# Expert-choice search in two halves of the latent tokens and the context side by side, with jobs of the attention and router stages in a new order (2 layers, float32, one core)

## The reference

```python
def trunk_layer(x, cvec, lp, lam_init, ctx_kv):
    mod = silu(cvec) @ lp['w_ada'] + lp['b_ada']            # 6 x 1024
    sh1, sc1, g1, sh2, sc2, g2 = split(mod, 6)
    h = rms_norm(x, lp['rms1_g']) * (1 + sc1) + sh1
    q, k, v, up, uc = split(h @ lp['w_in'])                 # 8 heads, 2 x 64 for q and k, 128 for v
    ...                                                     # q, k normed; rotary on latent tokens
    y_a = differential attention @ w_proj_a; y_b = pooling @ w_proj_b; y_c = convolution @ w_proj_c
    x = x + g1 * ((ga * y_a + gb * y_b + gc * y_c) @ lp['w_out'])
    h2 = rms_norm(x, lp['rms2_g']) * (1 + sc2) + sh2
    return x + g2 * expert_choice_ffn(h2, ...)

def expert_choice_ffn(h, w_router, w1, w3, w2):             # 16 experts, width 1024
    aff = softmax(h @ w_router)
    gate, idx = top_k(swapaxes(aff, 1, 2), cap)             # cap 64 of 512 latent, 16 of 128 context tokens
    xs = h[idx]
    ye = ((silu(xs @ w1) * (xs @ w3)) @ w2) * gate
    return scatter-add of ye at idx
```

## Time and profile before

| | |
|---|---|
| median of 3 runs | 2980.21 us (2978.73 to 2989.21) |
| the profiled execution | 2972.85 us, of which the span 2971.1 us |
| granted TensorE clock, mean | 0.973 of full speed |
| PE / PEld busy | 93% / 75% |
| DVE / ACT / POOL busy | 66% / 52% / 12% |
| chain that ended last | PE 68%, DMA 14%, DVE 8%, ACT 5%, issue 3% |
| stages of layer 0 (us) | start and input to 184, attention to 516, merge to 806, projection to 872, router to 920, experts to 1474 |
| stages of layer 1 (us) | attention 1644 to 1972, merge to 2262, projection to 2329, router to 2381, experts to 2938, end at 2971 |

### The profile page before, as it was taken

The page is one execution under the profiler, slowest core; times in us unless marked ns, Lnnn a source line. Parts: engine busy times, 40 slices in busy tenths (PEclk is TensorE's granted clock), DMA queues, the critical chain, the costliest instruction groups (busy, mean ns, idle before and its releaser), DMA issues.

```text
span 2971.1 us, 42113 instructions
## 1 busy us (share of the span) xinstructions
PE 2764.0 (93%) x17280; PEld 2238.3 (75%) x17280; DVE 1957.4 (66%) x2015; ACT 1547.5 (52%) x1993; POOL 365.4 (12%) x235
## 2 busy tenths in 40 slices
PE   6999997999988999999989999989999599999998
PEld 5988876999975666666679788779999466666666
DVE  2165656873438888888843666577534588888886
ACT  5235545324227777777642455543232377777774
POOL 0410110000011211111123011100000201111110
PEclk8999999999998999999999999989999799999999
DMA  7222232222268999999932233122232499999996
GB/s 242 89 85 90 93 92 80 70 80 100 79 221 306 374 375 372 373 375 375 341 125 72 79 107 103 51 90 82 67 104 100 165 316 374 375 371 374 375 372 239
DMA packets 373999, 605.63 MB, mean 204 GB/s; under 512 B 13040, under 2 KB 164720, under 8 KB 373040
## 3 DMA queue, kind: packets, MB, share of 16 engines
q1 hardware_dynamic: 360496, 551.67, 52.6%
q0 software_dynamic: 13312, 51.28, 5.6%
HBM read 572.62 MB, written 30.28 MB: 203 GB/s over the span
## 4 chain that ended last, share of the span: by engine, by line
PE 68%; DMA 14%; DVE 8%; ACT 5%; issue 3%; SPq 1%; DVEq 0%; ACTq 0%; POOLq 0%
PE ps L1351 20%; PE ps L1353 19%; PE ps L1352 19%; DMA m_raw<-in_w 11%; DVE m_lo L1271 2%; PE ps L1542 2%; PE ps L1575 2%; DMA raw<-in_w_ada 1%; ACT probs L546 1%; PE ps L1395 1%; DVE stats L1059 1%; PE ps L1564 1%; DMA xg<-h_rows,token_of_slot 1%; SPq L332 1%; DVE stats L1030 1%
## 5 line engine op out<-in xcount | busy, mean ns | idle before, releaser
L834 ACT CAST m_hi<-m_raw 128x2048 fp32r<-128x2048 f32 x384 | 732.9, 1912 | 292.5 <-DMA m_raw<-in_w 275.5
L1271 DVE TENSOR_TENSOR m_lo<-m_raw,m_hi 128x2048 fp32r<-128x2048 f32 x384 | 861.7, 2284 | 18.0 <-PE ps L1353 12.5
L1351 PE MATMUL ps<-h_hi,w_hi 128*128 128x384 f32 (+2 forms) x1408 | 439.5, 312 | 16.7 <-DVE h_lo L983 9.4
L1352 PE MATMUL ps<-h_lo,w_hi 128*128 128x384 f32 (+2 forms) x1408 | 436.8, 310 | 0.0
L1353 PE MATMUL ps<-h_hi,w_lo 128*128 128x384 f32 (+2 forms) x1408 | 436.8, 310 | 0.0
L1351 PE MATMUL ps<-m_hi,xs_hi 128*80 128x512 f32 x1024 | 406.1, 397 | 3.4 <-DVE xs_lo L1288 3.4
L1352 PE MATMUL ps<-m_lo,xs_hi 128*80 128x512 f32 x1024 | 403.8, 394 | 0.0
L1353 PE MATMUL ps<-m_hi,xs_lo 128*80 128x512 f32 x1024 | 403.2, 394 | 0.0
L1351 PE MATMUL ps<-w_hi,h_hi 128*128 128x256 f32 x960 | 283.0, 295 | 2.8 <-ACT pool_branch L673 1.8
L1351 PEld LDWEIGHTS ps<-h_hi,w_hi 128*128 128x128 f32 x1408 | 267.6, 190 | 22.0 <-issue 21.9
L1352 PE MATMUL ps<-w_lo,h_hi 128*128 128x256 f32 x960 | 273.7, 285 | 0.0
(11 more groups left out here) (292 smaller groups left out, 4632.7 us busy)
## 6 DMA issues: line engine op xcount, KB each, us to landing
m_raw<-in_w SPq DMA_DIRECT2D x384, 1024.0 KB, 10.3
raw<-in_w_in SPq DMA_DIRECT2D x72, 512.0 KB, 6.4
raw<-in_w_ada SPq DMA_DIRECT2D x64, 512.0 KB, 4.7
raw<-in_w_gate SPq DMA_DIRECT2D x48, 512.0 KB, 4.7
ada_in_a<-in_w_ada SPq DMA_DIRECT2D x10, 1024.0 KB, 11.9
raw<-in_w_proj_a SPq DMA_DIRECT2D x16, 512.0 KB, 4.0
raw<-in_w_out SPq DMA_DIRECT2D x16, 512.0 KB, 5.7
x_kept<-x POOLq DMA_DIRECT2D x2, 2560.0 KB, 10.4
```

The costliest lines, as they stand in the source:

```text
L834: nc.scalar.copy(m_hi[:, g % HIS], m_raw[:, g % RAWS]).then_inc(s["m_high"], 1)
L1271: nc.vector.tensor_tensor(m_lo[:, g % LOS], m_raw[:, g % RAWS], m_hi[:, g % HIS].bitcast(F32), ALU.subtract).then_inc(s["msplit"], 1)
L1351: pe.matmul(out, wh, xh, start=first, stop=False, skip_group_check=True)
L1352: pe.matmul(out, wh, xl, start=False, stop=False, skip_group_check=True)
```

## The change

- **Job tables, loads.** `a1` moves from the end of tile 3 to tile 4, behind the turns and the first part's scores; `v1` or `v4` moves from ahead of the turns to the place where `a1` was. In the last head all four modulation jobs come one or two tiles later. SP asks for the next head's chunks between the two modulation chunks of a head, no longer ahead of both.
- **Start of layer 0.** `ada_turned` runs in three parts among the last two chunks; `split_low(0, 0)` comes behind `add_mods` and `coefficients`.
- **Last chunk of the output projection.** Its second tile's third piece goes to bank 2, TensorE reports each tile by itself, VectorE and ScalarE take the first while the second is computed. A one-column exponential stands behind the root. VectorE fills four tiles with constants.
- **Search.** The affinities are laid out in 32-wide groups (two divisions instead of one) so that two transposes put the first 256 latent tokens on partitions 0 to 15, the other 256 on 32 to 47, the context on 64 to 79. Eight rounds run over 80 partitions by 256 columns. The two latent lists are laid against each other, the second reversed; after two transposes of 80 rows the larger value at each of the 64 places is taken, with its token. The 64 are then the right set, no longer in falling order.
- **Order behind the search.** On TensorE the wait for the search and the two transposes (now into bank 6, behind the wait for the last token rows' copies) come ahead of `ada_turned(l + 1, 4)`. On VectorE the three `low` come ahead of the next layer's `add_mods` and `coefficients`.

```diff
-EVEN = (("", "q1", "q2"), ("", "q3", "q4"), ("", "v0", "a0"), ("", "b0", "a1"), ("v1 tq tk tc", "", "Q0 b1"))
-ODD = (("", "q1", "q2"), ("", "q3", "q4"), ("", "v2", "a0"), ("", "v3", "b0 a1"), ("v4 tq tk tc", "", "Q0 b1"))
-LASTH = (("", "a0", ""), ("", "b0", "a1"), ("", "b1", ""), ("", "", ""), ("", "", ""))
+EVEN = (("", "q1", "q2"), ("", "q3", "q4"), ("", "v0", "a0"), ("", "b0", "v1"), ("tq tk tc", "a1", "Q0 b1"))
+ODD = (("", "q1", "q2"), ("", "q3", "q4"), ("", "v2", "a0"), ("", "v3", "b0 v4"), ("tq tk tc", "a1", "Q0 b1"))
+LASTH = (("", "", ""), ("", "a0", ""), ("", "b0", ""), ("", "a1", "b1"), ("", "", ""))
...
-                for h in range(HEADS):
+
+                def tiles_of(h):
+
                     if h % 2 == 0 and h < HEADS - 2:
                         wide(0, in_v[l, h // 2 + 1 + V0 // CW])
                     if h < HEADS - 2:
                         qk_chunk(h + 2)
                     elif h == HEADS - 2:
                         wide(0, gate_v[l, MERGE[0][1] + 4 * MERGE[0][0]])
-                    for a in (ADA0 + 2 * h + 1, ADA0 + 2 * h + 2):
-                        if a < 24:
-                            ada_chunk(a)
+
+                tiles_of(0)
+                for h in range(HEADS):
+                    ada_chunk(ADA0 + 2 * h + 1)
+                    tiles_of(h + 1)
+                    if h < HEADS - 1:
+                        ada_chunk(ADA0 + 2 * h + 2)
...
-                    squares(2 * c, 2 * c + 2)
-                seen("proj", 4)
+                    squares(2 * c, 2 * c + (1 if c == 3 else 2))
+                act.wait_ge(s["xo_done"], seen("xo_done"))
+                squares(KT - 1, KT)
+                seen("proj", 5)
 
                 root_of_rows()
+                nc.scalar.activation(st[:, 6:7], ones[:, 0:1], ACT.Exp)
...
-                    split_low(0, 0)
                     add_mods(0, 0)
                     coefficients(0, 8, "rms1")
+                    split_low(0, 0)
...
+                    if c == 3:
+                        nc.vector.memset(affw[:], -1.0)
+                        nc.vector.memset(top_f[:], 0.0)
+                        nc.vector.memset(top_w[:], 0.0)
+                        link(nc.vector.memset(aff_lanes[:], 0.0))
                     for j in range(2):
                         ct = 2 * c + j
+                        third = 2 if (c, j) == (3, 1) else 3 * u + 2
+                        if c == 3:
+                            dve.wait_ge(s["proj"], seen("proj"))
                         for col, a, e in ((1, 0, 3 * P), (1, 3 * P, LAT), (0, LAT, TOK)):
-                            src = ps[:, 3 * u + j, 0:3 * P] if a == 0 else ps[:, 3 * u + 2, 256 * j + a - 3 * P:256 * j + e - 3 * P]
+                            src = ps[:, 3 * u + j, 0:3 * P] if a == 0 else ps[:, third, 256 * j + a - 3 * P:256 * j + e - 3 * P]
                             ins = nc.vector.scalar_tensor_tensor(x[:, ct, a:e], src,
                                                                  mods_of[l][:, 16 + ct, col:col + 1], mm_[:, ct, a:e], ALU.mult, ALU.add)
+                        if (c, j) == (3, 0):
+                            seen("xo_done")
+                            ins.then_inc(s["xo_done"], 1)
...
-                nc.vector.tensor_tensor(aff[:], aff[:], st[:, 8:13].unsqueeze(2).to_broadcast([P, TT, EXPERTS]), ALU.mult).then_inc(s["aff_r"], 1)
+                turn = st[:, 8:13].unsqueeze(2).to_broadcast([P, TT, EXPERTS])
+                nc.vector.tensor_tensor(aff_lanes[:, 0:3, 0:EXPERTS], aff[:, 0:TT:2], turn[:, 0:TT:2], ALU.mult)
+                nc.vector.tensor_tensor(aff_lanes[:, 3:TT, 0:EXPERTS], aff[:, 1:TT:2], turn[:, 1:TT:2], ALU.mult).then_inc(s["aff_r"], 1)
...
-                nc.vector.tensor_copy(affw[:], flat[0:EXPERTS, 5 * 512:5 * 512 + TOK]).then_inc(s["aff_in"], 1)
+                nc.vector.tensor_copy(affw[0:64], ps[0:64, 5, 0:LAT // 2])
+                nc.vector.tensor_copy(affw[64:LANES, 0:CTX], ps[64:LANES, 5, 0:CTX]).then_inc(s["aff_in"], 1)
                 dve.wait_ge(s["aff_in"], seen("aff_in"))
-                for a, b, at, rounds in ((0, LAT, 0, CAP_LAT // 8), (LAT, TOK, CAP_LAT, CAP_CTX // 8)):
-                    for i in range(rounds):
-                        best = top_v[:, at + 8 * i:at + 8 * i + 8]
-                        link(nc.vector.max(best, affw[:, a:b]))
-                        link(nc.vector.max_index(top_i[:, at + 8 * i:at + 8 * i + 8], best, affw[:, a:b]))
-                        if i < rounds - 1:
-                            link(nc.vector.match_replace(affw[:, a:b], best, affw[:, a:b], -1.0))
-                nc.vector.tensor_copy(top_f[:, 0:CAP_LAT], top_i[:, 0:CAP_LAT])
-                nc.vector.tensor_scalar(top_f[:, CAP_LAT:], top_i[:, CAP_LAT:], float(LAT), None, ALU.add).then_inc(s["topk"], 1)
+                for i in range(CAP_LAT // 8):
+                    best = top_v[:, 8 * i:8 * i + 8]
+                    link(nc.vector.max(best, affw[:]))
+                    link(nc.vector.max_index(top_i[:, 8 * i:8 * i + 8], best, affw[:]))
+                    if i < CAP_LAT // 8 - 1:
+                        link(nc.vector.match_replace(affw[:], best, affw[:], -1.0))
+                nc.vector.tensor_copy(top_w[0:EXPERTS, 0:CAP_LAT], top_v[0:EXPERTS])
+                nc.vector.tensor_copy(top_w[32:32 + EXPERTS, 0:CAP_LAT], top_v[32:32 + EXPERTS, ::-1])
+                nc.vector.tensor_copy(top_w[64:LANES, CAP_LAT:], top_v[64:LANES, 0:CAP_CTX])
+                nc.vector.tensor_copy(top_f[0:EXPERTS, 0:CAP_LAT], top_i[0:EXPERTS])
+                nc.vector.tensor_scalar(top_f[32:32 + EXPERTS, 0:CAP_LAT], top_i[32:32 + EXPERTS, ::-1], float(LAT // 2), None, ALU.add)
+                nc.vector.tensor_scalar(top_f[64:LANES, CAP_LAT:], top_i[64:LANES, 0:CAP_CTX], float(LAT), None, ALU.add).then_inc(s["topk"], 1)
                 dve.wait_ge(s["posT"], seen("posT"))
-                nc.vector.tensor_copy(index[:], ps[0:SLOTS, 7, 0:EXPERTS])
-                nc.vector.tensor_copy(st[0:SLOTS, 62:63], ps[0:SLOTS, 7, EXPERTS - 1:EXPERTS])
-                nc.vector.tensor_copy(gates[:], ps[0:SLOTS, 7, EXPERTS:2 * EXPERTS]).then_inc(s["routed"], 1)
+                placed = ps[0:SLOTS, 6, 0:2 * LANES].rearrange("p (n c) -> p n c", n=2)
+                value_a, token_a = placed[0:CAP_LAT, 0, 0:EXPERTS], placed[0:CAP_LAT, 1, 0:EXPERTS]
+                value_b, token_b = half_b[:, 0], half_b[:, 1]
+                link(nc.vector.tensor_copy(half_b[:], placed[0:CAP_LAT, :, 32:32 + EXPERTS]))
+                nc.vector.tensor_tensor(a_or_b[:], token_a, token_b, ALU.subtract)
+                link(nc.vector.tensor_tensor(from_a[:], value_a, value_b, ALU.is_ge))
+                nc.vector.tensor_copy(token_f[CAP_LAT:], placed[CAP_LAT:, 1, 64:LANES])
+                link(nc.vector.tensor_tensor(a_or_b[:], a_or_b[:], from_a[:], ALU.mult))
+                link(nc.vector.tensor_tensor(token_f[0:CAP_LAT], a_or_b[:], token_b, ALU.add))
+                nc.vector.tensor_copy(index[:], token_f[:])
+                nc.vector.tensor_copy(st[0:SLOTS, 62:63], token_f[:, EXPERTS - 1:EXPERTS])
+                nc.vector.tensor_tensor(gates[0:CAP_LAT], value_a, value_b, ALU.max)
+                nc.vector.tensor_copy(gates[CAP_LAT:], placed[CAP_LAT:, 0, 64:LANES]).then_inc(s["routed"], 1)
...
+                dve.wait_ge(s["h2_out"], seen("h2_out", 16 * TT))
+                for g in range(AHEAD_LO):
+                    low(g)
                 if l < DEPTH - 1:
                     dve.wait_ge(s["small_in"], seen("small_in", 32))
                     add_mods(l + 1, 4)
                     coefficients(l + 1, 8, "rms1")
-                dve.wait_ge(s["h2_out"], seen("h2_out", 16 * TT))
-                for g in range(AHEAD_LO):
-                    low(g)
...
-                    ada_first(6, 8)
-                    ada_turned(0, 0)
+                    ada_turned(0, 0, 0, 2)
+                    ada_first(6, 7)
+                    ada_turned(0, 0, 2, 3)
+                    ada_first(7, 8)
+                    ada_turned(0, 0, 3, 4)
...
+                        if (c, j) == (3, 1):
+                            seen("proj")
+                            ins.then_inc(s["proj"], 1)
+                            pe.wait_ge(s["set_free0"], seen("set_free0", 0) + 1)
...
-                for c in range(TT):
-                    ins = pe.transpose(flat[0:EXPERTS, 5 * 512 + c * P:5 * 512 + (c + 1) * P], aff[:, c, :], ident[:])
+                pe.transpose(ps[0:96, 5, 0:P], aff_lanes[:, 0:3].rearrange("p t e -> p (t e)"), ident[:])
+                ins = pe.transpose(ps[0:64, 5, P:2 * P], aff_lanes[:, 3:TT].rearrange("p t e -> p (t e)"), ident[:])
...
+                pe.wait_ge(s["topk"], seen("topk"))
+                pe.wait_ge(s["h2tok"], seen("h2tok", 2))
+                seen.settle()
+                pe.transpose(ps[0:SLOTS, 6, 0:LANES], top_w[:], ident[0:LANES, 0:LANES])
```

(7 more changed lines are left out.)

34 lines of the change are left out of this document (22 added, 12 removed).

## The result

The changed kernel takes 2966.43 us (median of six runs, 2959.58 to 2972.10) where the kernel before, in six runs of the same measurement, takes 2985.55: 19.1 us less, a ratio of 0.9933 with a 95% interval of 0.9918 to 0.9949. The forecast was 18.6 us less and 2961.6 us. The total agrees, but three of its five terms don't: what two of them had too much is made good by a gain that the sum held open and by a rest that no stage explains.

The account below looks back on a forecast made before the run. TensorE was taken to bound the stages, with transfers at full share among the experts and sequential waits between stages. Start 4.4, attention 5, gather starts 5.1 and 4.1 made 18.6 us off 2980.21: 2961.6 us, range 2950 to 2977.

Parts of the forecast that it names:

- a gain that the sum held open: First gathers of the expert stages: one short and one long kept as before, 0 in the sum, bounds -5.5 and +5.5.
- The start: Layer 0's start: early turns fill waits, first modulated tile 4.4 us earlier; 1.5 if the clock falls before 37.
- Attention: Both layers' attention: moved jobs and loads remove waits for modulation chunks; 5 us gained, ends -1 and 10.
- the second rival: Attention: rotation replaces the chunk's wait and the clock falls there too; gain 0, total 2966.6 us; chance 0.13.
- The fear about SP's order: Heads 2 and 4, both layers: first modulation chunk asked for late, could wait; slower, 2995 us; chance 0.06.
- From the projection to the search: Each layer, end of output projection: split handover and early table load bring all that follows 3.0 us earlier.
- The search: Each layer's token search: 256-column maxima at 0.415 us; 7.9 of 19.2 us goes, six closing copies add 0.35.
- What is late then: Into the gathers: token-row stores decide, not the search; gather starts 5.1 us earlier in layer 0, 4.1 in layer 1.
- The gather's length: First gather of each layer, 8.05 and 13.61 us before: either length possible in either; one short, one long kept.
- The first rival: Both gathers alike: both long 2967.1 us, chance 0.10; both short 2956.1 us, chance 0.27.
- The sum: Whole kernel: 4.4 + 5 + 5.1 + 4.1 = 18.6 us gained, taken from the median, giving 2961.6 us.
- The premise: Expert stage: TensorE busy 544 of 554 us, transfers at full share; earlier first product brings the end forward as much.

Follow-up runs that it names:

- jobs_as_before: Changed kernel with the job tables and SP's load order of the kernel before put back: 2966.68 us, ratio to before 0.9940.
- rows_first: Changed kernel; layer 0's fourth to sixth expert chunk held until the gather landed, low parts until its issue, rows' low part and cast earlier: 2965.95 us.

## Why the prediction came out right, step by step

- **The start: right.** 4.4 us forecast, 4.6 measured at the first modulated tile, 3.9 between the second traces of the two kernels (46.73 and 42.84); at the first scores 4.6 and 3.2. The condition held too: the clock was still full during the early turns, 1.84 us for 16 of them, and, which the sum had not assumed, even at chunk 7.
- **Attention: wrong, 5 us forecast, none found.** The working of layer 1's head 0 was right: the turns start 38.17 us after the head's first scores instead of 38.85, and the head takes 40.65 instead of 41.30. What failed is the rest of the sum, which counted the half clock behind the old waits as saved. The new waits, for the rotation, are as long, and the clock falls as often (a mean of 0.94 to 0.97 over the stages of both traces before, 0.92 to 0.96 after): that is the second rival. It came true in full; that the measured time also meets its total, 2966.6 us, is luck, since that total has the other wrong terms in it. The prediction also left the last row of the table without a price. Counted from first scores to first scores, the first seven heads of both layers take 609.0 us together in the four traces with the old tables and 604.1 in the seven with the new ones (those averaged for `jobs_as_before`); the last heads take it back, 57.5 us and 64.0. These hold one modulation chunk more (161 products instead of 145), which now runs behind the boundary, and in the first traces their clock is 0.74 and 0.80 instead of 0.94 and 0.81. The fear about SP's order did not come true: no modulation chunk was late.
- **From the projection to the search: right in kind, 3.0 forecast.** Updates 2.18 to 1.14, squares 1.36 to 0.74, and from the last subtraction's start (879.65) to the exponential's 0.33 us instead of 1.61: 2.9 together. The stretch in the table got another 0.9 shorter, in TensorE's small steps between, which I did not cost: behind a wait of 0.87 us for ScalarE's square, which had been 2.54, they ran at a granted clock of 0.95 (874 to 880 us) instead of 0.53 (873 to 880).
- **The search: right, and in the shade as forecast.** 0.424 us for a maximum against 0.415 estimated; from the first maximum's start to the last index's start 11.1 us instead of 18.9. It is not the search that releases the gathers.
- **What is late then: right in layer 1, wrong in layer 0.** In layer 1 from the first update to the gather's start 83.17 became 78.93, 4.2 us against 4.1 forecast (5.1 between the second traces), released by the last store as worked out. In layer 0 84.24 became 82.78: 1.5 instead of 5.1 (1.7 between the second traces). The step that failed is "lands a median 3.5 later (3.0 to 4.2)". That landing time was read where the expert chunks had all but arrived; moved ahead, the last store is issued 6.6 us before the sixth chunk lands, and takes 8.39. In every trace with the changed order the landing stays 34.2 to 34.5 us behind the chunks' issue, unless the loads themselves are held. That point was named in no rival.
- **The gather's length: the wrong kind of uncertainty.** I kept one short and one long and called it open. Both are short, 5.3 us saved on average in layer 1, and not by chance: the release decides, and the change moved it from VectorE's slots to the stores. The first rival's "both short" had it. With it the Trainium skill (SBUF — State Buffer, Who interferes with whom) is to be weighed again: it infers that a subtraction with two SBUF inputs leaves descriptor writing alone. The prediction read the trace as speaking against that; the runs don't. Plain issues take 0.55 us beside such subtractions, and only the indirect one, which reads its row numbers from SBUF, is held up: 0.98 us without a subtraction beside it, 2.3 to 2.8 or 6.6 with. Whether it is that reading which waits was not tested.
- **The sum.** 4.6 + 0 + 1.5 + 4.2 + 5.3 = 15.6 us from the traces; 15.8 by the second ones; measured 19.1, with an interval of 0.9918 to 0.9949, that is 15.2 to 24.5. The two agree, but 3.5 us are not accounted for. They belong to no stage of the traces: the mean spans of the two traces of each kernel differ by 14.8 us, so it is the untraced executions that differ by more. Forecast term by term the same list was 4.4 + 5 + 5.1 + 4.1 + 0 = 18.6: 5 and 3.6 us too much are made good by 5.3 that stood only in a rival and by the unexplained rest.
- **The premise** that an earlier first product is an earlier end holds in layer 1 and failed in layer 0 as soon as it was used in earnest (`rows_first`): there TensorE and the queues are both near their limit, and chunks that come later cost what the rows had won.

## What to carry to other kernels

Read a transfer's landing time together with what else was in the queues at that moment, and count from the event that loaded them: a distance that stays under edits of the code between (here 34.2 to 34.5 us in the changed kernels) tells that more such edits won't help. Look at each kernel by itself: the kernel before had the same distance with the loads already landed. Where an indirect DMA is issued from POOL, keep VectorE's instructions on two SBUF tiles away from the moment of its issue; here half a microsecond of fills was worth 5 us. And trace both kernels twice before believing a stage that has a clock in it.

## What the runs showed of the hardware that I had not expected

- A gather of 80 rows that is issued undisturbed takes 0.98 us on POOL and lands 3.9 to 4.0 us after its start; behind one subtraction 2.3 to 2.8 and 8.0 to 8.7 (5.5 with no chunk load in flight, 9.6 beside three held ones); behind three 6.6 and 13.1 to 13.6. Among the first gathers of the layers those that begin up to 0.84 us after the first subtraction's start end behind that one, those that begin 0.92 us or more after it behind the third. That is no general limit: of the changed kernel's later gathers the one at 1252.30, 0.50 us after a subtraction's start, ends behind that one, those at 1145.33 and 2775.85, 0.55 and 0.67 us after, behind the next. What decides it is open.
- The last of five stores of 512 KB takes 3.7 to 4.4 us to land in a free queue and 7.3 to 8.4 beside the loads of expert chunks. The Trainium skill (DMA: Bandwidth & Descriptors, Queues, rings and completion order) has each DMA engine take turns among its queues; the changed kernel's layer 0 agrees with that, since the sixth chunk takes 21.2 us there instead of 16.9 and lands 1.8 us before the last store.
- The search instructions cost by columns and not by partitions, as far as three forms show it: 80 partitions by 256 columns take 0.424 us, 0.01 off the line between 0.282 for 128 and 0.682 for 512 on 16 partitions.
- The changed kernel's attention stage of layer 0 took 339 us in one execution and 331 in the next, that of layer 1 329 in both, with VectorE, ScalarE and GpSimd busy for the same time within 0.5 us: the granted clock alone. Its mean over the stage was 0.92 in the slowest of these and 0.96 in the fastest.
